# Four transformer layers on one core: three 256 wide matmuls per weight block instead of a 512 and a 256 wide one, one PSUM bank per pair of output tiles, the norm's scale put into VectorE's eviction

## The reference, cut to what matters

```python
# first block, layer 0 (even mixer: attention and gated linear attention), layer 1 (odd mixer: recurrent)
h = h + mixer(rms_norm(h, mix_g))            # projections ev_in, ev_out | od_xr, od_gate, od_ax, od_out
h = h + conv_ffn(rms_norm(h, ffn_g))         # up0/down0, up1/down1
#   conv_ffn: t = 3 tap causal conv(x @ w_up) + b;  u, g = split(t);  (u * gelu(g)) @ w_down
x = rms_norm(h, final_g)
# second block, twice
x = x + 0.5 * rms_norm(swiglu(rms_norm(x, pre1)), post1)                        # upA, downA
x = x + rms_norm(hybrid(rms_norm(x, mpre)), mpost)                              # bg .. w_o
x = x + 0.5 * rms_norm(swiglu(rms_norm(x, pre2)), post2)                        # upB, downB
#   swiglu: g, u = split(x @ w_gate_up);  (silu(g) * u) @ w_down
#   hybrid: z = x @ w_in; y_a = (b_g * conv3(c_g * v)) @ w_conv_out
#           y_p = pool_mixer(p) @ w_pool_out; (sig(ga) * y_a + sig(gp) * y_p) @ w_o
# rms_norm(x, g) = x * rsqrt(mean(x * x) + 1e-6) * g
```

## Time and profile before

| | |
|---|---|
| median of three runs | 2149.6 us (2149.39 to 2150.0) |
| profiled execution, first to last instruction | 2155.6 us |
| mean granted TensorE clock in it | 0.942 |
| TensorE (PE) busy | 1906.1 us, 88% |
| VectorE (DVE) busy | 1502.4 us, 70% |
| ScalarE (ACT) busy | 1094.9 us, 51% |
| GpSimd (POOL) busy | 557.1 us, 26% |

### The profile page before, as it was taken

One profiled execution on the slowest core, in us unless ns is written; L12 is line 12 of the kernel. 1 busy time (PEld: TensorE's weight loads), 2 busy tenths in 40 slices (PEclk: granted clock), 3 DMA queues, 4 the chain that ended last, 5 costly groups with the idle time before them and its releaser, 6 DMA issues.

```text
span 2155.6 us, 29622 instructions
## 1 busy us (share of the span) xinstructions
PE 1906.1 (88%) x10322; PEld 1619.9 (75%) x10322; DVE 1502.4 (70%) x1815; ACT 1094.9 (51%) x1380; POOL 557.1 (26%) x243
## 2 busy tenths in 40 slices
PE   7869888996788888999888989998999888989996
PEld 6747666775676677888777768886888777877885
DVE  5886666665866665886676678866786676577875
ACT  5524555446555544554445545554554445555554
POOL 3300444113044410220265202210220264202210
PEclk9969999998799999999899999998999899998998
DMA  6313333533233344555344443453556344543553
GB/s 253 114 39 120 124 136 136 185 147 117 101 133 136 136 158 155 175 180 210 138 155 159 173 176 137 178 212 138 175 185 222 122 154 160 191 156 130 184 217 131
DMA packets 46735, 336.92 MB, mean 156 GB/s; under 512 B 5184, under 2 KB 5568, under 8 KB 5952
## 3 DMA queue, kind: packets, MB, share of 16 engines
q1 hardware_dynamic: 46512, 335.34, 42.8%
q0 software_dynamic: 144, 0.52, 0.1%
HBM read 334.80 MB, written 1.05 MB: 156 GB/s over the span
## 4 chain that ended last, share of the span: by engine, by line
PE 56%; DVE 14%; POOL 13%; issue 10%; ACT 4%; ACTq 1%; DVEq 1%; DMA 0%; POOLq 0%; SPq 0%
PE psum L252 36%; PE psum L255 18%; POOL scratch L357 12%; DVE scratch L267 3%; DVE w_lo L236 2%; DVE scratch L589 2%; ACT scratch L536 2%; ACT scratch L264 1%; DVE scratch L1140 1%; POOL scratch L1291 1%; PE psum L291 1%; DVE scratch L397 1%; DVE x_split L326 1%; DVE scratch L1336 1%; DVE scratch L1212 1%
## 5 line engine op out<-in xcount | busy, mean ns | idle before, releaser
L252 PE MATMUL psum<-x_split,w_hi 128*128 128x512 f32 x3272 | 1204.6, 410 | 125.3 <-DVE w_lo L236 52.3
L255 PE MATMUL psum<-x_split,w_lo 128*128 128x256 f32 x3272 | 935.8, 286 | 0.0
L252 PEld LDWEIGHTS psum<-x_split,w_hi 128*128 128x128 f32 x3272 | 634.8, 194 | 303.3 <-issue 81.3
L236 DVE TENSOR_TENSOR w_lo<-w_raw,w_hi 128x2048 fp32r<-128x2048 f32 x315 | 813.8, 2585 | 23.9 <-ACT w_hi L228 23.9
L357 POOL TENSOR_TENSOR scratch<-scratch,inv_rms 128x512 f32<-128x512 f32 (+1 forms) x196 | 479.4, 2448 | 984.7 <-DVE scratch L267 812.9
L228 ACT ACTIVATE w_hi<-w_raw 128x2048 fp32r<-128x2048 f32 x316 | 603.0, 1909 | 126.1 <-PE psum L255 120.7
L252 PE MATMUL psum<-h_split,w_hi 128*128 128x512 f32 x1664 | 598.8, 403 | 54.9 <-DVE h_split L1266 21.1
L255 PEld LDWEIGHTS psum<-x_split,w_lo 128*128 128x128 f32 x3272 | 638.8, 195 | 0.4
L255 PE MATMUL psum<-h_split,w_lo 128*128 128x256 f32 x1664 | 471.2, 283 | 0.0
L252 PEld LDWEIGHTS psum<-h_split,w_hi 128*128 128x128 f32 x1664 | 317.3, 191 | 139.6 <-issue 27.4
L267 DVE TENSOR_TENSOR scratch<-psum,scratch 128x512 f32<-128x512 f32 x261 | 179.6, 688 | 325.5 <-ACT scratch L264 325.4
(11 more groups left out here) (176 smaller groups left out, 816.1 us busy)
## 6 DMA issues: line engine op xcount, KB each, us to landing
w_raw<-stream_in SPq DMA_DIRECT2D x316, 1024.0 KB, 4.8
x_resid<-x_in SPq DMA_DIRECT2D x1, 1024.0 KB, 7.1
y_out<-x_resid SPq DMA_DIRECT2D x1, 1024.0 KB, 3.9
scratch<-mask_in SPq DMA_DIRECT2D x1, 768.0 KB, 13.0
scratch<-ev_in SPq DMA_DIRECT2D x1, 512.0 KB, 11.6
scratch<-inv_in POOLq DMA_DIRECT2D x1, 512.0 KB, 4.2
params<-par_in SPq DMA_DIRECT2D x1, 247.0 KB, 7.3
matrices<-mat_in SPq DMA_DIRECT2D x1, 192.0 KB, 9.0
```

The lines of the kernel that those rows point to most:

```text
L236: dve.tensor_tensor(w_lo[:, slot, :], raw[:, slot, :], w_hi[:, slot, :].bitcast(F32), ALU.subtract).then_inc(lo_ready, 1)
L252: pe.matmul(ps[:, bank, :], w_hi[:, c.slot, b:b + P], src[:, k0 + k, :, :].rearrange("p a t -> p (a t)"), start=first and k == 0, stop=False)
L255: done = pe.matmul(ps[:, bank, T:2 * T], w_lo[:, c.slot, b:b + P], src[:, k0 + k, 0, :], start=False, stop=last and k == nk - 1)
```

## The change

`multiply` issues three matmuls of 256 columns for a block, all on the same 256 columns of PSUM. The two tiles of a pair lie side by side in one bank. `take_hi`, `take_lo`, `scale_pool` and their semaphores are gone. `take_scaled` on VectorE reads the bank, multiplies by rinv and writes SBUF. `taken`, the ring of three pairs and TensorE's waits stay as they were.

```diff
@@ multiply
-                    bank = 2 * pair + m
-                    pe.matmul(ps[:, bank, :], w_hi[:, c.slot, b:b + P],
-                              src[:, k0 + k, :, :].rearrange("p a t -> p (a t)"),
-                              start=first and k == 0, stop=False)
-                    done = pe.matmul(ps[:, bank, T:2 * T], w_lo[:, c.slot, b:b + P],
-                                     src[:, k0 + k, 0, :], start=False, stop=last and k == nk - 1)
+                    dst = ps[:, pair, m * T:(m + 1) * T]
+                    pe.matmul(dst, w_hi[:, c.slot, b:b + P], src[:, k0 + k, 0, :],
+                              start=first and k == 0 and m == 0, stop=False)
+                    pe.matmul(dst, w_hi[:, c.slot, b:b + P], src[:, k0 + k, 1, :],
+                              start=False, stop=False)
+                    done = pe.matmul(dst, w_lo[:, c.slot, b:b + P], src[:, k0 + k, 0, :],
+                                     start=False, stop=last and k == nk - 1 and m == tiles - 1)
...
+        def take_scaled(dve, c, dst, tiles=2):
+            dve.wait_ge(chunk_done, c.number + 1)
+            dve.tensor_tensor(dst, bank(c.slot, tiles), rinv[:, :].unsqueeze(1).to_broadcast([P, tiles, T]),
+                              ALU.mult).then_inc(pair_taken, 1)
@@ out_dve
-                dve.wait_ge(*tr["half"].count(g + 1, l))
-                take_lo(dve, pair, half[:, :, :] if dst is None else S(dst + 2 * g, 2))
+                dve.wait_ge(chunk_done, c.number + 1)
                 if dst is None:
-                    dve.wait_ge(*taken(event))
                     xg = x[:, 2 * g:2 * g + 2, :]
-                    dve.tensor_tensor(xg, xg, half[:, :, :], ALU.add).then_inc(*tr["x"].one())
+                    dve.tensor_tensor(xg, bank(pair), xg, ALU.add).then_inc(pair_taken, 1)
+                else:
+                    dve.tensor_copy(S(dst + 2 * g, 2), bank(pair)).then_inc(pair_taken, 1)
@@ up_dve (the stages of a norm are all like this: chunk 0 is taken once rinv is there)
             for c in chunks(dve, phase, n, l, peel=3):
                 at = c.n if isinstance(c.n, int) else n
-                dve.wait_ge(*tr["half"].count(c.n + 1, l))
-                take_lo(dve, c.slot, S(PRE + 2 * c.slot, 2))
-                if at > 1:
-                    hidden(c, 1)
-                refill_lo(dve, c)
                 if at == 0:
                     chunk0 = c
+                    refill_lo(dve, c)
                     rinv_dve(dve, pre, l)
                     continue
                 if at == 1:
+                    dve.wait_ge(*pre["stat"].after("copied", l))
+                    take_scaled(dve, chunk0, S(PRE + 2 * chunk0.slot, 2))
+                    refill_lo(dve, c)
+                    take_scaled(dve, c, S(PRE + 2 * c.slot, 2))
+                else:
+                    take_scaled(dve, c, S(PRE + 2 * c.slot, 2))
+                    refill_lo(dve, c)
+                if conv:
+                    if at == 1:
+                        taps(chunk0, 0)
+                        continue
+                    if at == 2:
+                        taps(c, 1)
+                    taps(c, 0)
+                elif at > 1:
...
@@ up_pool (new: gating of up0 and up1 on GpSimd; steady chunk: lo(c, 2), then hidden(c, 1))
+            def hidden(c, prev):
+                s = (c.slot - prev) % RING
+                pool.wait_ge(*tr["up"].count(c.n + 1 - prev, l))
+                pool.wait_ge(*tr["act"].count(c.n + 1 - prev, l))
+                pool.tensor_tensor(S1(HID + s), S1(ACC + 2 * s), S1(GEL + s), ALU.mult)\
+                    .then_inc(*tr["hidden"].one())
+            def lo(c, prev):
+                s = (c.slot - prev) % RING
+                pool.wait_ge(*tr["hi"].count(c.n + 1 - prev, l))
+                pool.tensor_tensor(hs[:, bass.ds(c.n - prev, 1), 1, :], S(HID + s),
+                                   hs[:, bass.ds(c.n - prev, 1), 0, :].bitcast(F32), ALU.subtract)\
+                    .then_inc(*tr["lo"].one())
@@ odd_act (od_ax: sigmoids straight from PSUM, banks 3 to 5)
-                take_hi(act, pair, S(TMP + 2 * pair, 2)).then_inc(*A.did(f"ahalf{j}"))
-                act.wait_ge(*taken(E0["od_ax"] + j))
                 for t, (dst, b, nm) in enumerate(((RR, "ba", "r"), (II, "bx", "i"))):
-                    act.activation(S1(dst + j), S1(TMP + 2 * pair + t), ACT.Sigmoid,
+                    act.activation(S1(dst + j), ps[:, 3 + j % 3, t * T:(t + 1) * T], ACT.Sigmoid,
@@ hybrid_dve (pool_in, cv: no wait for GpSimd's scale; conv_out, pool, pool_out read PSUM in the operation itself)
-                dve.wait_ge(*scaled(c))
+                dve.wait_ge(*taken(c.event))
...
-                take_lo(dve, c.slot, S(YA + 2 * g, 2))
...
-                dve.tensor_tensor(S(YA + 2 * g, 2), S(YA + 2 * g, 2), S(GA + 2 * g, 2), ALU.mult)\
-                   .then_inc(*CO["ya"].one())
+                dve.tensor_tensor(S(YA + 2 * g, 2), bank(c.slot), S(GA + 2 * g, 2), ALU.mult)\
+                   .then_inc(pair_taken, 1)
```

More of the change, by code:

```diff
@@ L41 @@
 FIRST = [("ev_in", 13, 13), ("ev_out", 4, 4), ("up0", FF1, FF1), ("down0", 12, 4),
[L42 removed]
+         ("od_xr", 4, 4), ("od_gate", 4, 4), ("od_ax", 2, 0), ("od_out", 4, 4),
          ("up1", FF1, FF1), ("down1", 12, 4)]
@@ L46 @@
          ("w_o", 4, 4), ("upB", FF2, FF2), ("downB", 12, 4)]
-SCALED = ("ev_in", "up0", "od_xr", "od_gate", "up1", "upA", "bg", "pool_in", "cv", "gates", "upB")
-C0, E0, S0 = {}, {}, {}
-_c = _e = _s = 0
+C0, E0 = {}, {}
+_c = _e = 0
 for _name, _nc, _ne in FIRST:
-    C0[_name], E0[_name], S0[_name] = _c, _e, _s
-    _c, _e, _s = _c + _nc, _e + _ne, _s + (_ne if _name in SCALED else 0)
+    C0[_name], E0[_name] = _c, _e
+    _c, _e = _c + _nc, _e + _ne
 FIRST_CHUNKS = _c
 for _name, _nc, _ne in LAYER:
-    C0[_name], E0[_name], S0[_name] = _c, _e, _s
-    _c, _e, _s = _c + _nc, _e + _ne, _s + (_ne if _name in SCALED else 0)
+    C0[_name], E0[_name] = _c, _e
+    _c, _e = _c + _nc, _e + _ne
 LAYER_CHUNKS = _c - FIRST_CHUNKS
 LAYER_EVENTS = sum(n for _, _, n in LAYER)
-LAYER_SCALED = sum(n for name, _, n in LAYER if name in SCALED)
 CHUNKS = FIRST_CHUNKS + LAYERS2 * LAYER_CHUNKS
@@ L345, in pre_pe @@
                         rinv_pe(pe, tr, l)
-        def scale_pool(pool, phase, n, dst, l, tr=None):
-            if tr is not None:
-                pool.wait_ge(*tr["stat"].after("copied", l))
-                pool.sem_inc(pool_waited, 1)
-            for c in chunks(pool, phase, n, l):
-                pool.wait_ge(*taken(c.event))
-                if not isinstance(c.n, int):
-                    pool.sem_inc(pool_waited, 1)
-                pair = dst(c)
-                pool.tensor_tensor(pair, pair, rinv[:, :].unsqueeze(1).to_broadcast([P, pair.shape[1], T]),
-                                   ALU.mult).then_inc(pair_scaled, 1)
         def post_tracks(name, layered=True):
```

289 lines of the change are left out of this document (122 added, 167 removed).

## The result

The kernel after took 2044.27 us in the median of four runs (2042.35 to 2046.41), the kernel before 2149.8 us beside it. The ratio is 0.9509, with a 95% interval of 0.9491 to 0.9528: 105 us less. The forecast was 2035 us, in a range of 1957 to 2120.

The account below looks back on a forecast made before the run. TensorE bound some stages; up0 was held by a loop of latencies through GpSimd's scale, with no engine full. Terms from -76 (up0, up1) to +15 (new wait) summed to -115 us: 2149.6 - 115 = 2035 us, range 1957 to 2120.

Parts of the forecast that it names:

- The loop of latencies: up0 and up1: GpSimd's scale, taps and eviction follow one another; without the scale the period falls from 7.81 to 5.9 us, -76 us.
- the three matmuls: Every block: three 256 wide matmuls at 117 ns make 351 ns against 350, +5 us over 4936 blocks.
- the condition that I had set: Prediction counts as wrong if the block is not within 345 to 357 ns, or up0 takes over 155 us.
- Rival 1: Every matmul pays 20 ns of its own: block 380 ns against 351, 143 us more, time 2178; chance 0.12.
- new wait: Chunk 2 of a norm stage waits for pair 0's eviction with rinv: 1.7 us each, nine stages counted, +15 us.
- the clock: Stops of about 2 us at times lower the granted clock, 0.35 us each: +3 us.
- The odd mixer: od_ax loses copies and additions, -10 us; od_xr and od_gate wait less, -6; sum -16 us.
- cv and gates: 16 chunks would take 90 us, not 107; pool_in's means still collide, so -10.5 per loop turn, -21 us.
- pool to w_o: Pool stage's four steps and pool_out's last step lose copy and addition: -4.5 us per turn, -9 us.
- down0 and down1: First chunks of down0 still wait for VectorE's late w_lo; -5 us for each stage, -10 us.
- The bounds: Forecast's own bounds: up period 5.65 or 6.09 us (-12, +9), slots of 113 to 120 ns (-59, +44).

## Why the prediction was right

**The loop of latencies** was the step that carried the sum, and it held: up0 and up1 gave 81.7 us (forecast 76), and putting GpSimd's operation back gave the old period to the hundredth. I had left 0.25 us per chunk to GpSimd standing ahead of VectorE's taps (5.9 against 5.65 for TensorE). The taps did grow, by 1.0 us, but VectorE's chunk, 0.69 + 2.28 + 2.64 = 5.6, just stayed below the 5.76 that TensorE's took. The move of the gating to GpSimd, which the forecast counted as a relief of VectorE, was none.

**The term that was mis-sized is the three matmuls.** I wrote "3 x 117 = 351 ns against 350, +5 us". The slot is 120 and the block 360: 10 ns by 4936 blocks, up to +49. That breaks the condition that I had set (345 to 357). The wrong inference was that a new slot costs what the 256 wide slot of before does: that slot (113, 117 and 120 ns in turn, 117 on average) always stood behind a 512 wide one, and I spread the excess of a block over its columns. The excess belongs mostly to the matmul: about 13 ns each, 27 to 33 in the old block of two and 40 in the new one of three. Rival 1 had the right mechanism (a cost for each matmul, whatever its width) with the wrong size, 20 ns instead of 13.3; it decides from 374 ns on, and 360 is in between. Beside 256 columns the runs have 13.3 ns with 128 weight columns and 6.6 with 80 or fewer. The Trainium skill ("TensorE: Matmul & The Clock Gate", section "Back-to-back issue gap") has 2.5 ns over the columns, but gives that formula for an isolated matmul and says that in a stream of weight loads and matmuls both set the distance; the prediction applied it to such a stream. That the load enters agrees with the runs here.

**Why the sum came out nevertheless.** Against the profiled execution it was -115, and the two spans differ by 2155.6 - 2041.7 = -113.9. That it is so close is luck, because errors cancelled. The stages that TensorE bound before grew by 26 us (forecast 11): this is the dearer third matmul. The stages that waited for other engines gave 141 us. Their forecasts in the table add up to 134, and to 126 with their 5 us of new wait and the 3 us for the clock. Some 6 us of this difference are the steady period of up0 and up1, taken at 5.9 and measured at 5.76 (40 chunks); there the longer blocks cost nothing beyond the 5.76. In the medians an error of 9 us is left. It comes from the step from the span to the median: the profiled execution of before lay 6.0 us above its median, the one of after 2.6 below, and I had carried the 6.0 over. Later runs of the kernel before lie between 2140.9 and 2160.2 us, so 6 us are within what one execution differs from another.

**The new wait** lasted 1.9 to 2.1 us in each of the ten places, rinv's two matmuls included, for a forecast of 1.7. Its removal gave 14.6 us in all for the 15 in the sum, which had nine of them; in od_xr, the tenth, it brought nothing. Here the forecast can be checked alone, and it is right.

**The odd mixer, cv and gates, pool to w_o, down0 and down1** came within 3 us each. In cv the amount was right and the wait only in part. The forecast named the wait for the last of the means as what would be left of the loss. In the trace VectorE waits 1.85 us for the means of the last group but one, and TensorE's stop of 3.07 us is for a w_lo behind that wait, behind the window sums and in a collision; the low part of the last group comes after the stop. The run with another order took the stop away and gave 8.6 us.

**The bounds.** Those of the up period (-12, +9) take 48 chunks where the sum takes 40; with 40 they are -10 and +8. It changes nothing, since the range was set wider than the bounds.

**The clock.** The +3 us for stops that lower it did not show: upA, with the new wait, has 0.98 as before. In up0, where the stop in every period went, the granted clock rose from 0.94 to 1.00, and the mean of the whole program from 0.942 to 0.960. The gain of this is inside the stages' differences.

Not tried: the old form in up0 and up1, where VectorE's chunk of 5.6 us has no room for a second operation on a pair.

## What to carry to other kernels

When an operation sits in a loop of handovers between engines, its whole length counts even though no engine is full; look for the row whose releaser is the row before, all around the period, and take the slowest link out. Splitting one wide matmul into two narrow ones isn't free when TensorE is the bound: measure the distance of starts of the form that you will issue, not that of a like one in a mixed sequence. Once TensorE was the bound here, moving vector work between engines changed nothing, and the order around the few stops was what still paid.

## What the runs showed of the hardware that was not expected

- Float32 matmuls in the fp32r format with 128 x 128 weights started columns / 2.4 GHz + 13.3 ns apart with 256, 320, 384 and 512 columns, + 11.7 with 288 and + 16.0 with 448, and no closer than 111 ns with 128 to 240.
- At the lower clock they started 213 ns apart with 128 columns as with 256. In the run with widths up0 began at full clock, with 111 ns. From 206.6 us on, behind the eight one-column matmuls of the mean and without a stop of TensorE, the distance was 213. The granted clock then stayed at 0.50, the level of 1.2 GHz, though TensorE was busy for 138.74 of 140.00 us:

```profile
210.00:350.00 140.00, 138.74 (x649) 138.02 (x649) 75.30 (x86) 51.23 (x72) 20.03 (x25) 0.50 0.27 98
```

- Beside 256 columns, weights of 80 columns or fewer made a slot 6.7 ns shorter than 128 columns did, and 16 columns no more than 80.
- VectorE's taps (two operands in SBUF) took 1.67 us for four without GpSimd beside them and 2.64 with two GpSimd operations of 0.74 and 0.92. The eviction from PSUM with rinv kept its 0.68 to 0.69 us also where a GpSimd operation ran beside it (ten times, once at 1002.65 above). The rule of the Trainium skill ("SBUF — State Buffer", section "Who interferes with whom"), that a VectorE operation with two SBUF inputs contends with a GpSimd one that reads SBUF, and a VectorE operation like this eviction, with one SBUF input, does not, agrees with both.
